# HGRN scores with narrower weights and decode outer products in one matmul per half: one decoder step on one core

## What is computed

```
def hgrn2_chunkwise(q, log_f, k, i, s0):       # blocks of the sequence
    cum = cumsum(log_f)                        # within the block
    wdec = exp(where(causal, cum[l] - cum[m], -inf))
    att = einsum('bhld,bhlmd,bhmd->bhlm', q, wdec, k)        # scores
    o = att @ i + (q * exp(cum)) @ s
    s = exp(last)[..., None] * s + einsum('bhld,bhle->bhde', k * exp(last - cum), i)
```

## Time and profile before

| | |
|---|---|
| median of 3 runs | 3384.95 us (3381.28 to 3386.05) |
| the profiled execution | 3388.75 us |
| its span, first to last instruction | 3386.9 us |
| mean granted TensorE clock | 0.938 |
| PE busy | 3111.2 us, 92% |
| PE weight loads busy | 2737.9 us, 81% |
| DVE / ACT / POOL busy | 1446.3 / 1025.7 / 1044.8 us |

### The profile page before, as it was taken

How to read it: one execution, slowest core, us unless ns; L and a number is a source line. 1 busy time by engine, 2 the same in 40 slices (tenths; PEclk the granted TensorE clock), 3 DMA queues, 4 the chain that set the end, 5 groups by cost and what they waited for, 6 DMA issues and landing times. The chain is left out here.

```text
span 3386.9 us, 46400 instructions
## 1 busy us (share of the span) xinstructions
PE 3111.2 (92%) x16972; PEld 2737.9 (81%) x16972; DVE 1446.3 (43%) x2909; ACT 1025.7 (30%) x1726; POOL 1044.8 (31%) x662
## 2 busy tenths in 40 slices
PE   6999899799999687689699988999979999996999
PEld 6999899688888575489588857999978888886886
DVE  7998344214420497543300004124345544446442
ACT  4111122312211242433200002024445344455741
POOL 2223222132223364010212211245425344345432
PEclk9999999899999898799799998999979998997899
DMA  5444655455543563443522213333334333333343
GB/s 131 102 127 130 186 170 159 109 131 167 167 127 93 182 211 125 158 130 93 210 75 99 99 60 100 88 120 116 115 104 147 96 126 125 104 99 134 125 134 107
DMA packets 372318, 430.06 MB, mean 127 GB/s; under 512 B 45488, under 2 KB 314416, under 8 KB 362976
## 3 DMA queue, kind: packets, MB, share of 16 engines
q1 hardware_dynamic: 258448, 360.43, 33.9%
q10 hardware_dynamic: 113744, 67.91, 6.7%
HBM read 281.07 MB, written 151.39 MB: 128 GB/s over the span
## 5 line engine op out<-in xcount | busy, mean ns | idle before, releaser
L1114 PE MATMUL p_psum<-p_h_hi,p_w_hi 128*128 128x344 f32 (+1 forms) x1600 | 568.3, 355 | 0.0
L1114 PE MATMUL p_psum<-p_h_hi,p_w_lo 128*128 128x344 f32 (+1 forms) x1600 | 562.2, 351 | 0.0
L1114 PE MATMUL p_psum<-p_h_lo,p_w_hi 128*128 128x344 f32 (+1 forms) x1600 | 560.9, 351 | 0.0
L2489 PE MATMUL p_psum<-p_h_hi,p_w_hi 128*128 128x344 f32 (+1 forms) x1280 | 465.6, 364 | 0.0
L2489 PE MATMUL p_psum<-p_h_lo,p_w_hi 128*128 128x344 f32 (+1 forms) x1280 | 458.5, 358 | 0.0
L2489 PE MATMUL p_psum<-p_h_hi,p_w_lo 128*128 128x344 f32 (+1 forms) x1280 | 458.2, 358 | 0.0
L698 POOL CAST p_w_hi<-p_w_raw 128x1024 fp32r<-128x1024 f32 x80 | 88.8, 1110 | 820.6 <-PE p_psum L1114 683.2
L1114 PEld LDWEIGHTS p_psum<-p_h_hi,p_w_hi 128*128 128x128 f32 x1600 | 302.9, 189 | 36.5 <-issue 9.3
L1114 PEld LDWEIGHTS p_psum<-p_h_hi,p_w_lo 128*128 128x128 f32 x1600 | 302.8, 189 | 29.0
L1114 PEld LDWEIGHTS p_psum<-p_h_lo,p_w_hi 128*128 128x128 f32 x1600 | 302.9, 189 | 28.5
L2254 DVE COPY p_out<-p_psum 128x344 f32<-128x344 f32 (+1 forms) x160 | 93.6, 585 | 489.5 <-PE p_psum L2489 489.4
(11 more groups left out here) (328 smaller groups left out, 5915.2 us busy)
## 6 DMA issues: line engine op xcount, KB each, us to landing
p_w_raw<-in_w_in SPq DMA_DIRECT2D x144, 512.0 KB, 4.7
z<-p_out ACTq DMA_DIRECT2D x64, 512.0 KB, 3.5
z<-p_out SPq DMA_DIRECT2D x64, 512.0 KB, 3.2
p_raw<-z SPq DMA_DIRECT2D x32, 1024.0 KB, 5.5
rt_raw<-z SPq DMA_DIRECT2D x16, 1536.0 KB, 7.0
c_m_raw<-m SPq DMA_DIRECT2D x16, 1024.0 KB, 7.0
p_xt<-x SPq DMA_DIRECT2D x32, 512.0 KB
u_s<-p_out SPq DMA_DIRECT2D x128, 73.0 KB, 3.2
```

Source lines behind the costliest of these rows:

```text
L1114: ins = pe.matmul(bank, wv[par][:, k, :], h[:, k, c0:c0 + n], start=(k == 0 and j == 0), stop=(k == KD - 1 and j == 2))
L2489: ins = pe.matmul(bank, wv[par][:, k, :], h[:, k, c0:c0 + n], start=(k == 0 and j == 0), stop=(k == KD - 1 and j == 2))
```

## The change

Scores: the matmul of sub-block j takes only the first m = 32(j+1) columns of its keys as weights and writes only m rows of PSUM. The rows below m are not written any more; the bank is zeroed once by VectorE (`zero_done`), and PE waits for that in its first tile. The two fills of `k_ref` go.

Decode: keys and values swap roles. The keys are copied as they are (`k_own`, 8 x 128) and are the weights; the values are spread block-diagonally (`i_own`, 8 rows x 1024 columns, in `wrow`). One matmul with 512 moving columns does the four outer products of a call.

```diff
-        k_own = wrow[0:NS].rearrange("p (n c) -> p n c", c=P)
+        i_own = wrow[0:NS]
-        i_own, o_all = sb("i_own", [NS, P]), sb("o_all", [NS, HH, P])
+        k_own, o_all = sb("k_own", [NS, P]), sb("o_all", [NS, HH, P])
@@ VectorE, before the strips
-            for par in range(2):
-                dve.memset(k_ref[par][:], 0.0)
+            dve.memset(ps_score, 0.0).then_inc(zero_done, 1)
@@ VectorE, own_keys
-                dve.tensor_copy(i_own[:], ps_own[0:NS, 0, :])
-                dve.tensor_tensor(k_own, bcast(ps_own[0:NS, 1, :], 1, NS), bcast(ident[0:NS, 0:NS], 2, P), ALU.mult)\
+                dve.tensor_copy(k_own[:], ps_own[0:NS, 1, :])
+                dve.tensor_tensor(i_own.rearrange("p (n c) -> p n c", c=P), bcast(ps_own[0:NS, 0, :], 1, NS),
+                                  bcast(ident[0:NS, 0:NS], 2, P), ALU.mult)\
                     .then_inc(own_done, 1)
@@ PE, scores
                 if n:
                     pe.wait_ge(sc_done, n)
+                else:
+                    pe.wait_ge(zero_done, 1)
                 for h in range(H4):
                     for j in range(NSUB):
-                        cols = slice(j * SUB, (j + 1) * SUB)
-                        ins = pe.matmul(ps_score[:, h, cols], k_ref[par][:, j, h, :], q_ref[par][:, h, cols],
+                        cols, m = slice(j * SUB, (j + 1) * SUB), SUB * (j + 1)
+                        ins = pe.matmul(ps_score[0:m, h, cols], k_ref[par][:, j, h, 0:m], q_ref[par][:, h, cols],
                                         start=True, stop=True)
@@ PE, own_states
-                for b in range(4):
-                    ins = pe.matmul(ps_kv[:, b, :], k_own[:, 4 * c + b, :], i_own[:], start=True, stop=True)
-                ins.then_inc(kv_mm, 1)
+                pe.matmul(ps[:, 3, :], k_own[:], i_own[:, BLK * c:BLK * (c + 1)], start=True, stop=True)\
+                    .then_inc(kv_mm, 1)
```

More of the change, by code:

```diff
@@ L1776, in project_hgrn @@
         xi, xo, sq = xt, xn, [o[:, 0:D] for o in out_buf]
-        const_ld = sem("const_ld")
+        const_ld, zero_done = sem("const_ld"), sem("zero_done")
         x_ld, w_ld, stored = ([sem(f"{n}{i}") for i in range(2)] for n in ("x_ld", "w_ld", "stored"))
```

## The result

The changed kernel takes 3394.99 us, the median of 7 runs (3391.02 to 3405.78), against 3386.05 (3381.28 to 3390.82) for the kernel before; the ratio is 1.0028, 95% interval 1.0016 to 1.0040. That is some 9 us slower. The forecast was 3392, seven above the median of 3384.95 it started from. The profiled execution took 3394.99 us too, 6.3 us more in its span than before.

What follows compares the result with a forecast made beforehand. PE's instruction stream was taken to bound the HGRN part. Scores +5.7, decode -0.2 and clock +1.6 sum to +7.1 us, 3392 from the median 3384.95; the forecast's own range 3384 to 3401, overall range 3374 to 3408.

Steps and rivals of the forecast that it cites:

- Loads: Score weight loads on PE: shorter with fewer columns, 110, 137, 165 and 192 ns; alone 42 us less over 32 tiles.
- Changes of shape: Scores on PE: three drains a head at 0.119 us outweigh the shorter loads; +0.20 us a tile, +5.7 us after corrections.
- The third change: Within a head's scores, weights going from 32 to 64 columns: taken to cost a full drain, 0.119 us.
- the fourth: Within a head's scores, weights going from 96 to 128 columns: taken as free; its full price would be 15 us.
- (a): Scores: 32 to 64 columns costs no drain, 15 us less over 32 tiles, 3377 us; chance 0.12.
- (b): Scores: no change of shape drains, as the streams are so short; -38 us, 3347 us; chance 0.07.
- Rival (d): Scores: the drain waits for the predecessor's whole record, 0.28 us; +29 us, 3421 us; chance 0.07.
- 3.7 us: Sign in a tile's timeline: the stage from first score to L2517 takes 3.7 us where it was 3.49.
- The low clock: Scores of a tile at the lower PE clock: 6.8 us before and 6.8 after, no difference.
- Decode: Outer products, 16 calls: one 512-column matmul for four, 1.26 us a call instead of 1.28; -0.2 us in all.
- The clock: Falls of PE's granted clock behind transposes and scores: one more fall, +1.6 us, bounds -5 and +12.
- rival (c): Clock falls behind the scores in more tiles and stays low longer; eight more make +12 us, about 3403; chance 0.13.

Runs made afterwards that it cites:

- e3: The full change with the two score loops exchanged, so all four heads of one width come before the next width: 3335.27 us, ratio 0.9847 to the kernel before.
- e4: The change with score weights of 66, 66, 96 and 128 columns and the `k_ref` fills back: 3327.30 us, ratio 0.9828 to the kernel before.
- e5: The change with score weights of 64, 64, 96 and 128 columns and the `k_ref` fills back: 3384.30 us, ratio 0.9985 to the kernel before.
- e1: The change's narrower score weights alone, decode outer products as in the kernel before: 3395.34 us, ratio 1.0034 to the kernel before.
- e7: The kernel before with each tile's scores cut in two, heads 2 and 3 moved behind a dense block: 3350.51 us, ratio 0.9898 to the kernel before.

## Why the prediction was right

**What bounds.** PE's own stream set the end of the main loop, as forecast: no wait appeared or went with the change, and a step at full clock grew by what its stage grew. In the kernels with a much shorter stage this no longer holds to the full: e3 and e4 wait 12 and 11 us more.

**Loads.** 0.11, 0.13, 0.16, 0.19 us for 32 to 128 columns, forecast 110, 137, 165 and 192 ns. The saving is real: e4, with weights a little wider and no drain, takes 0.99 us off a tile.

**Changes of shape.** The step that decided the sign. The third change, 32 to 64, which no row of before showed, costs the same as the others (e5 and the loader's starts); the fourth, 96 to 128, costs nothing (the head takes 0.92 us). That nothing was, by the prediction's own rows, the nearer of two guesses worth 15 us; it came out, and the rows had not shown it. Rivals (a) and (b) fell. 0.119 was the estimate of a drain with the short stream before it; e3 gives 0.116. Rival (d), a drain that lasts as long as the record, fell with it. The tile came out 0.18 us longer, forecast 0.20; 5.8 us over 32 tiles, forecast 6.4 before corrections. One of the signs was worked out wrong: "3.7 us" from the first score to L2517. The prediction's own 3.78 from the last transpose, less the 0.20 ahead of the first score, gives 3.58, and 3.58 is what tile 4 shows (2432.91 to 2436.49; before 2426.59 to 2430.09, 3.50); for rival (a) the sum gives 3.1, not 3.2.

**The low clock.** Here the prediction was wrong: it put 6.8 us for a tile before and after, and tile 23 took 6.9 and 6.2. The starts of that tile's single records after the change show which term was too dear. The loads are as forecast (0.161 us from 96 to 128 columns, 0.213 between the two records of 128), but a head takes 1.48 us: with 1.08 for the loads, 0.40 is left for three changes of shape, 0.13 each. The prediction had a drain of 0.14 and 0.053 of stream besides. By its own 8% of tiles at the low clock this is some 2 us in the change's favour.

**Decode.** 0.03 us a call, forecast 0.02. **Zeroing:** nothing, as forecast.

**The clock.** The mis-sized term. I gave it 1.6 us, with -5 to +12 as bounds. Stage and decode leave some 4 us of the 9 between the medians, within those bounds but more than I took. The profiled pair says as much. From the first score to that of tile 22, the last ahead of PE's long wait, it took 755.12 us before (2303.19 to 3058.30) and 761.79 after (2302.72 to 3064.51), 6.7 more. By the traces' clock records 6.8 us more of that time are at the lower level, and half of that, 3.4, is lost; the other 3.3 are PE's own. In e1 it is 8.4 us more, 5.1 of them by the clock and again 3.3 PE's own. This is a net figure of falls that come and go. The first four tiles, before and after:

```profile
2303.19:2426.59 123.40, 123.40 (x846) 123.33 (x845) 45.99 (x104) 61.96 (x120) 55.90 (x45) 0.97 0.35 110
```

```profile
2302.72:2432.91 130.19, 130.19 (x845) 127.57 (x845) 45.94 (x104) 61.95 (x120) 55.98 (x45) 0.92 0.33 104
```

They are 6.8 us longer, and four stages are only 0.7 of it. That is what rival (c) describes; but from tile 18 to tile 24 the change is 4.0 us shorter than the kernel before (173.16 and 169.18 us, clock 0.83 and 0.86). One execution of each doesn't say how much of the medians' 9 us is the clock's. So part of the closeness of 3392 to 3394.99 is luck: PE's own part came out a little smaller than forecast, the clock's larger, and the two errors offset each other in part.

What I did miss is the size of the whole effect. I took the falls as something that comes and goes with shifts, and priced one more of them; in fact taking most of them from the kernel before gains 33 us, net of some 4 us more waiting for others (e7), and the experiments that shortened the stage by a sixth to somewhat over a quarter got 20 to 27 us that I had not expected of them. For the change this was harmless, since its stage grew by only a twentieth.

**Better than both.** 66, 66, 96 and 128 columns (e4) keep the shorter loads, pay no drain and shorten the thin stretch: 3327.30 us, 1.7% below the kernel before. Cutting the scores on top of that adds nothing measurable (3325.62).

## What to carry to other kernels

Before narrowing the weights of plain fp32 products, find in a trace what a change between widths costs beside the load that it saves: here 0.12 us a change against 0.16 us that the narrowest product saves with its two loads. Order products by width, or keep all of them at 66 columns or more; here both turned the same idea from +0.3% into -1.5% and -1.7%. And where PE never waits, look at the granted clock of the loop: a long row of products with few columns can slow the dense work behind it, here by about 1 us a tile beside a row of 3.6 us. Cutting the row in two cost no instruction and gained 33 us in the kernel before, with some 4 us of added waiting already taken off; behind the 66-column weights it gained nothing.

## What the runs showed of the hardware that I had not expected

Products with weights of 66 columns start 0.11 us after the transposes and those with 64 columns 0.20, so two columns more are quicker by 0.09 us (e4 and e5). And the same instructions in an order that puts dense matmuls between two short rows of thin ones raised the granted clock in 460 us of the loop from 0.93 to 1.00 and took 33 us from 3383 (e7). At the lower clock the change's tile is the quicker one, 6.2 us against 6.9, where at full clock it is the slower, 3.78 against 3.60.
